# A decoder trunk's feed-forward layers on one Trainium2 core: three plain tile pairs in place of four, and another order of work at the start of the up projection

## The reference

```python
x = x + rms_norm(mixer(rms_norm(x, mix_pre)), mix_post)
x = x + rms_norm(conv_glu_ffn(rms_norm(x, ffn_pre), w_up, conv_w, w_down), ffn_post)

def conv_glu_ffn(h, w_up, conv_w, w_down):
    u = causal_depthwise_conv(h @ w_up, conv_w)      # three taps, along the tokens
    gate, val = jnp.split(u, 2, axis=-1)             # 2816 channels each
    return (jax.nn.silu(gate) * val) @ w_down
```

## Time and profile before

| | us |
|---|---|
| median of 3 runs | 2617.52 (2615.26 to 2622.68) |
| the profiled execution | 2618.37 |
| its span in the trace | 2616.9 |
| TensorE busy | 2543.2 (97%) |
| VectorE busy | 1644.4 (63%) |
| GpSimd busy | 1311.1 (50%) |
| ScalarE busy | 1189.5 (45%) |

### The profile page before, as it was taken

How to read it: one execution, slowest core, us unless ns; L and a number is a source line. 1 busy time by engine, 2 the same in 40 slices (tenths; PEclk the granted TensorE clock), 3 DMA queues, 4 the chain that set the end, 5 groups by cost and what they waited for, 6 DMA issues and landing times. The chain is left out here.

```text
span 2616.9 us, 34537 instructions
## 1 busy us (share of the span) xinstructions
PE 2543.2 (97%) x12557; PEld 2104.3 (80%) x12557; DVE 1644.4 (63%) x1797; ACT 1189.5 (45%) x1738; POOL 1311.1 (50%) x843
## 2 busy tenths in 40 slices
PE   7899999999999999999999999999998999999998
PEld 5788888888777788888887788888887888888887
DVE  5677666777166766667328657557457666676327
ACT  6445445545443444444446434434543444444444
POOL 2454335353511777775668111111502778775667
PEclk9999999999999999999999999999999999999999
DMA  3234444334543232323766211011523223234666
GB/s 136 61 115 138 128 124 133 84 120 117 143 136 110 77 109 89 116 98 116 242 226 201 90 40 42 32 51 41 168 95 109 86 93 117 93 104 158 217 214 217
DMA packets 123391, 313.06 MB, mean 120 GB/s; under 512 B 13472, under 2 KB 27360, under 8 KB 119936
## 3 DMA queue, kind: packets, MB, share of 16 engines
q1 hardware_dynamic: 119936, 288.31, 32.4%
q0 software_dynamic: 3328, 23.07, 4.6%
HBM read 247.33 MB, written 110.13 MB: 137 GB/s over the span
## 5 line engine op out<-in xcount | busy, mean ns | idle before, releaser
L559 POOL TENSOR_TENSOR f_wlo<-f_raw,f_whi 128x512 fp32r<-128x512 f32 x154 | 267.8, 1748 | 131.7 <-ACT f_whi L642 131.6
L516 POOL TENSOR_TENSOR f_wlo<-f_raw,f_whi 128x512 fp32r<-128x512 f32 (+1 forms) x120 | 189.6, 1580 | 254.9 <-ACT f_whi L611 254.9
L943 DVE TENSOR_TENSOR f_wlo<-f_raw,f_whi 128x512 fp32r<-128x512 f32 x154 | 152.1, 999 | 176.2 <-ACT f_whi L642 176.1
L642 ACT ACTIVATE f_whi<-f_raw 128x1024 fp32r<-128x1024 f32 x154 | 162.8, 1060 | 204.2 <-PE f_value L83 102.7
L516 POOL TENSOR_TENSOR f_wlo<-f_sums,f_whi 128x512 fp32r<-128x512 f32 x144 | 193.2, 1363 | 37.7 <-ACT f_whi L611 37.7
L685 ACT ACTIVATE f_kept<-f_part 128x512 f32<-128x512 f32 x108 | 64.5, 597 | 168.1 <-PE f_part L83 164.0
L2060 POOL TENSOR_TENSOR g_wlo_first<-g_raw_first,g_whi_first 128x1024 fp32r<-128x1024 f32 x15 | 36.7, 2444 | 183.0 <-ACT g_whi_first L2154 183.0
L611 ACT ACTIVATE f_whi<-f_sums 128x512 fp32r<-128x512 f32 x144 | 86.0, 624 | 87.2 <-POOL f_sums L522 87.2
L3088 POOL TENSOR_TENSOR l_wlo<-l_raw,l_whi 128x1024 fp32r<-128x1024 f32 x12 | 29.4, 2447 | 179.8 <-ACT l_whi L3118 179.8
L81 PE MATMUL banks<-x_hi,g_whi_first 128*128 128x512 f32 x256 | 110.1, 430 | 3.9 <-POOL g_wlo_first L2060 3.9
L83 PE MATMUL f_part<-x_hi,f_wlo 128*128 128x512 f32 x288 | 113.4, 394 | 0.0
(11 more groups left out here) (596 smaller groups left out, 8246.9 us busy)
## 6 DMA issues: line engine op xcount, KB each, us to landing
f_raw<-in_ffn_w_up SPq DMA_DIRECT2D x88, 512.0 KB, 3.8
f_raw<-operands_of SPq DMA_DIRECT2D x154, 256.0 KB, 2.8
f_raw<-w_sums SPq DMA_DIRECT2D x88, 256.0 KB, 3.0
w_sums<-in_ffn_w_down POOLq DMA_DIRECT2D x28, 768.0 KB, 8.3
f_raw<-in_ffn_w_down SPq DMA_DIRECT2D x66, 256.0 KB, 4.1
operands_of<-f_hid SPq DMA_DIRECT2D x22, 512.0 KB, 2.8
w_sums<-in_ffn_w_down SPq DMA_DIRECT2D x14, 768.0 KB, 7.7
w_sums<-w_sums SPq DMA_DIRECT2D x14, 768.0 KB, 6.7
```

Of the source, the lines that this page charges most:

```text
L516: pool.tensor_tensor(part_of(w_lo, k), source, part_of(w_hi, k).bitcast(F32), ALU.subtract) \
L559: pool.tensor_tensor(step_part(w_lo, more_lo, d)[:, far], source[:, far], step_part(w_hi, more_hi, d)[:, far].bitcast(F32), ALU.subtract). ...
L642: act.activation(step_part(w_hi, more_hi, d)[:, :], (raw + [last_raw])[r][:, :], ACT.Copy).then_inc(s_hi, 1)
L943: dve.tensor_tensor(step_part(w_lo, more_lo, d)[:, near], source[:, near], plain32(step_part(w_hi, more_hi, d)[:, near]), ALU.subtract).th ...
```

## The change

`PLAIN` becomes 3: the fourth pair too is made from seven products. The start of the up projection is written out in a new order on ScalarE and on VectorE, with the gate's convolution ahead of the other token sums, and the low parts of the four plain weight tiles that are left move from GpSimd to VectorE (`plain_low`). `ready` waits for an older convolution where the value's other home is used. In the last four steps of the down projection (`SHARED`) VectorE splits all 1024 columns and GpSimd none. In `mixer_tail` the first five blocks of `half_product` stand ahead of the turns that are left over, and in layer 0 three turns stand behind other blocks.

```diff
-PLAIN = 4
+PLAIN = 3
+    SHARED = STEPS - 4
@@ SyncE: load_step, store rows, the next stage's first load
-                sp.wait_ge(s_lo, FIRST_DOWN + d - FFN_RAWS)
+                sp.wait_ge(s_lo, FIRST_DOWN + min(d - FFN_RAWS, SHARED))
-            if p >= PLAIN:
+            elif p > PLAIN:
@@ GpSimd
-        for n in range(2, 2 * PLAIN):
-            low(n, raw[n % FFN_RAWS][:, :])
         for s in s_rstore:
             pool.wait_ge(s, 16)
+        pool.wait_ge(s_lo, 2 * PLAIN)
...
         for d in range(STEPS):
-            step_low(d)
+            if d < SHARED:
+                step_low(d)
@@ ScalarE (the loop over the plain pairs goes)
+        high(2)
+        scaled_gate(0)
+        high(3)
+        token_sum_high(0, t1_hi[:, 0:2, :])
+        silu(0)
+        scaled_value(0)
+        token_sum_high(1, t2_hi[:, 0:2, :])
+        high(4)
+        token_sum_high(2, t4_hi[:, 0:2, :])
+        scaled_gate(1)
+        token_sum_high(3, t1_hi[:, 2:4, :])
+        high(5)
+        silu(1)
+        scaled_value(1)
+        high_operands(PLAIN, A11)
+        token_sum_high(4, t2_hi[:, 2:4, :])
+        high_operands(PLAIN, S1, S2)
+        token_sum_high(5, t4_hi[:, 2:4, :])
+        scaled_gate(2)
+        token_sum_high(6, x_hi[:, 0:2, far])
+        high_operands(PLAIN, A12)
+        token_sum_high(7, x_hi[:, 2:4, far])
+        high_operands(PLAIN, S3, A22)
+        silu(2)
+        scaled_value(2)
@@ VectorE (the loop over the plain pairs goes)
+        def plain_low(n):
+            dve.wait_ge(s_hi, n + 1)
+            dve.tensor_tensor(part_of(w_lo, n), raw[n % FFN_RAWS][:, :], plain32(part_of(w_hi, n)), ALU.subtract) \
+                .then_inc(s_lo, 1)
...
+                cols = near if d < SHARED else slice(0, T)
...
         first_difference(0)
+        plain_low(2)
+        conv(0, gate_ps, gate)
+        first_low(0)
+        second(0)
+        plain_low(3)
+        conv(1, value_ps[0], hid[0])
+        activated(0)
+        second_low(0)
+        fourth(0)
+        first_difference(1)
+        plain_low(4)
+        conv(2, gate_ps, gate)
+        fourth_low(0)
+        first_low(1)
+        plain_low(5)
+        conv(3, value_ps[1], hid[1])
+        activated(1)
+        for kind in (R_F, R_D, R_S, R_G):
+            row_sum(kind, 0)
+        second(1)
+        fourth(1)
+        second_low(1)
+        third_difference(0)
+        fourth_low(1)
+        third_low(0)
+        third_difference(1)
+        third_low(1)
+        conv(4, gate_ps, gate)
+        conv(5, value_ps[0], hid[0])
@@ TensorE
         def ready(n):
             pe.wait_ge(s_lo, n + 1)
-            if n >= 2:
+            if n >= 2 and n % 2 == 0:
                 pe.wait_ge(s_conv, n - 1)
+            elif n >= 5:
+                pe.wait_ge(s_conv, n - 3)
@@ mixer_tail, TensorE
+            pe.wait_ge(s_post, place(NT - 2) + 1)
+            pe.wait_ge(s_free, max(place(t) for t in range(NT // 2)) + 1)
+            follows.half_product(pe, range(0, 5))
             for n in range(turned_tiles, NT - 1):
                 turn(n)
-            pe.wait_ge(s_post, place(NT - 2) + 1)
-            pe.wait_ge(s_free, max(place(t) for t in range(NT // 2)) + 1)
-            follows.half_product(pe, range(KT))
+            follows.half_product(pe, range(5, KT))
@@ layer 0's turns
-                          (((), (5,)), ((3,), (3,)), ((1, 5), (3,))),
+                          (((), (5,)), ((3,), (3,)), ((2,), (0, 5))),
```

More of the change, by code:

```diff
@@ L502, in _ @@
             if t == NT // 2 and lead is not None:
-                sp.wait_ge(s_lo, FIRST_DOWN + STEPS)
+                sp.wait_ge(s_lo, FIRST_DOWN + SHARED)
                 sp.wait_ge(s_hlo, STEPS)
@@ L600, in _ @@
             lead.small_low(pool)
-            pool.wait_ge(s_lo, FIRST_DOWN + STEPS)
+            pool.wait_ge(s_lo, FIRST_DOWN + SHARED)
             lead.low(pool)
@@ L942, in hidden_low @@
                 source = (raw + [last_raw])[d % (FFN_RAWS + 1)]
-                dve.tensor_tensor(step_part(w_lo, more_lo, d)[:, near], source[:, near],
-                                  plain32(step_part(w_hi, more_hi, d)[:, near]), ALU.subtract).then_inc(s_hlo, 1)
+                cols = near if d < SHARED else slice(0, T)
+                dve.tensor_tensor(step_part(w_lo, more_lo, d)[:, cols], source[:, cols],
+                                  plain32(step_part(w_hi, more_hi, d)[:, cols]), ALU.subtract).then_inc(s_hlo, 1)
         def value_far(p):
@@ L961, in rows_of @@
         def rows_of(q):
-            if q == PLAIN:
-                row_sum(R_F, q // 2 - 1)
             if q % 2:
                 row_sum(R_F, q // 2)
-                row_sum(R_G, q // 2 - 1)
+                if q > PLAIN:
+                    row_sum(R_G, q // 2 - 1)
             else:
@@ L1203, in step_ready @@
         def step_ready(d):
-            pe.wait_ge(s_lo, FIRST_DOWN + d + 1)
+            pe.wait_ge(s_lo, FIRST_DOWN + min(d + 1, SHARED))
             pe.wait_ge(s_hlo, d + 1)
```

## The result

The changed kernel takes 2628.36 us in the median of 6 runs (2627.67 to 2629.85), the kernel before 2619.03 (2615.26 to 2622.68): a ratio of 1.0033, 95% interval 1.0021 to 1.0044, 9.3 us slower. The forecast was 2625.0: 7.7 above the 2617.5 that was known of the kernel before when it was made, 6.0 above its median here. The profiled execution has a span of 2627.0, 10.1 more than before.

A forecast was written before the change was run, and what follows sets the result against it. TensorE, busy 97%, was taken as the bound, so only fewer matmuls or less idling help. Terms 3.2 + 3.4 + 2.2 - 1.4 + 0.3 = +7.7 us gave 2625.2 against the median, rounded to 2625.0; range 2610 to 2633.

The forecast's parts named there:

- mixer's end: Layer 0, before the up projection: a turn no longer hidden, bank late, +1.1, slower clock after idling +1.1; sum +2.2 us.
- The first wait goes: Second gate of the first pair, both layers: TensorE's idle 5.02 and 6.36 us and the slow clock after them disappear.
- What is late next: Up projection, S2 of pair 3: TensorE idles 12.8 us for ScalarE's kept copy; +3.2 us layer 0, +3.4 layer 1.
- The list: VectorE's instructions from the up projection's start through `conv(4)`: 61.1 us undisturbed, 69.1 with GpSimd's interference.
- meetings: Up projection: VectorE's and GpSimd's instructions delay each other; each costs VectorE 1.0 us, eight cost 8, bounds 0 to 12.9.
- half clock: TensorE runs at clock 0.50 after idling: 1.8 us taken before S2, 1.1 before the half product, between 0 and 2.15.
- Rivals 1, 2 and 3: VectorE's list: GpSimd not in the way, 2609 (0.17); whole instructions waited for, 2635 (0.12); first wait stays, 2632 (0.08).
- 84 matmuls: Up projection: the one more pair of seven behind the late S2, 19.35 us, before the place answering to the old S2.
- The ends of the down projections: Last splits, full width on VectorE: -1.4 us in layer 0 (-2.3 to +2.1), +0.3 in layer 1 (-0.6 to +1.5).

The follow-up runs named there:

- last splits alone: Changed kernel with only the last four splits of each down projection shared again between VectorE and GpSimd, as in the kernel before: 2628.40 us.
- fewer meetings: Changed kernel with GpSimd's last two sums and low part of A12, first pair of seven, held until VectorE's last token sum has its low part: 2623.33 us.
- GpSimd light: Changed kernel with GpSimd's instructions for the first pair of seven cut from 512 to 8 columns, leaving out that computation: 2612.72 us.
- three pairs with these together: Changed kernel with the mixer's end as before, first kept copy earlier on ScalarE, and GpSimd's last instructions for the first pair of seven held: 2620.16 us.

## Why the prediction was right

The sum, by the same landmarks (VectorE's first instruction, S2 of pair 5, the first matmul of layer 1's mixer, the end of the span):

| step | forecast | measured |
|---|---|---|
| up to VectorE's start, layer 0 (mixer's end) | +2.2 | +3.96 (3.2 of it the mixer's end) |
| up projection, layer 0 | +3.2 | +2.9 |
| down projection, layer 0 | -1.4 | -0.5 |
| mixer of layer 1 | 0 | -1.2 |
| up projection, layer 1 | +3.4 | +4.1 |
| down projection, layer 1 | +0.3 | +0.9 |
| sum | +7.7 | +10.1 (of the span) |

The measured column is of one profile against one. Its -1.2 in a mixer where nothing was changed is scatter: that stretch takes 517.2 us in the kernel before, 516.0 in the changed one, and 517.1 to 517.8 in the runs with four pairs, with the mixer's end as before and with the last splits as before. It hides about a third of what the other steps lie above the forecast, so that the sum is nearer than its terms is luck.

- **The first wait goes**: right; the gate follows without idle time in both layers.
- **What is late next**: right in place and size. The list was added up to 61.1 us; without meetings it is 862.64 - 800.92 = 61.7. Eight meetings at 1.0 were forecast and eight of 0.99 measured; `conv(4)` at 69.1, as forecast; the wait 12.6 and 12.7 for 12.8. The half clock behind it cost 1.78 and 2.2 for 1.8; that this is so near is partly luck, since the same wait cost 2.8 in another run (last section). Rivals 1, 2 and 3 fall with these numbers. One place is misread without harm to the sum: between S2 of the first pair of seven and S2 of the next lie 16.6 us (902.99 - 886.39 in the kernel before), not 84 matmuls, so S2 of pair 4 comes at 890.48, only 0.1 later than VectorE's start explains; the 84 matmuls and the 3.2 us are right at S2 of pair 5, which the table takes.
- **The mixer's end**: the mechanism right, the half clock mis-sized. Its 15 matmuls take 787.65 - 782.54 = 5.11 us, 1.65 more than 15 x 0.2304, where 1.1 had been taken between 0 and 2.15. With the turn's 0.8 us and 0.3 ahead of the second half that is 2.7 of the 3.2 us; the rest has no cause that was shown. The other 0.8 us of the table's step is no more than the scatter of VectorE's start among the traces with the old end (796.4 to 797.2 in seven of eight).
- **The ends of the down projections**: of the gain of 1.4 in layer 0 only 0.5 is there, and the run with the last splits alone does not tie that to the splits. VectorE's four take 5.73 us, in the forecast's bounds of 4.9 to 9.0, but TensorE still waits 1.5 us for them and 1.2 for another result of VectorE's; layer 1's seven take 14.14, the upper end of the forecast's 10.1 to 14.1.
- **What the sum hides**: the change is two large effects of opposite sign, -19 us for the order and about +25 for the count, plus 2 to 3 for the mixer's end. The forecast of +7.7 had them together, and only the runs with one of them show that the order was worth keeping without the count.

## What to carry to other kernels

Fewer matmuls in front of a product whose operand another engine makes are no gain when that engine's list does not shrink with them: TensorE lost 22 us of plain work in front of S2, VectorE's list 7.7 (76.9 against 69.1, meetings included). Before leaving out work on the busiest engine, add up the list of the engine that releases the next wait, with its meetings with GpSimd, and see which one is longer. And take apart a change of several edits: the four pairs in the new order, at 2601.26, beat both kernels.

## What the runs showed of the hardware

- The price of half clock did not follow the idle time. Against 0.2304 us each, fifteen matmuls took 1.4 us more after 9.61 us of idle time (870.41 to 875.28, fewer meetings), 2.1 after 4.56 and after 8.00, 2.9 after 4.71 (layer 1 with GpSimd light), 2.4 after 16.26 (880.39 on), and after 12.6 us 1.8 in the changed kernel but 2.8 with the plain splits on GpSimd (871.14 to 877.38). Behind the mixer's end it was 1.65 after 3.85. Shorter waits cost little in some cases and not in others: 12 matmuls took 0.1 more after 1.19 and 2.23 us, 1.7 more after 2.67 (the last two in the two layers of the run of three pairs with these together). So the cuts that left a wait of over 4 us gave back its idle time and, as far as the scatter of 1.4 to 2.9 lets one see, nothing of the clock.
- Meetings cost VectorE 0.99 us when GpSimd's instruction takes 1.30 alone, and up to 1.75 when it takes 2.42. Convolutions, which read one input from PSUM, took 1.28 us inside GpSimd's splits as well as alone. The Trainium skill, "SBUF — State Buffer", section "Who interferes with whom", says that a VectorE instruction with at most one SBUF input, outside the modes that use both of its port pairs, does not contend with GpSimd; the row at 804.48 agrees.
